# Token rows laid out turned by the host, and modulated there by per-partition columns

## The reference

```python
sh1, sc1, g1, sh2, sc2, g2 = split(silu(c) @ w_mod + b_mod, 6)          # latent tokens
csh1, csc1, ...            = split(silu(c_ctx) @ w_mod + b_mod, 6)      # context tokens
modulate(x, g, shift, scale) = rmsnorm(x, g) * (1 + scale) + shift
h_lat, h_ctx = modulate(x, g_attn, sh1, sc1), modulate(ctx, g_attn, csh1, csc1)
z  = h @ w_in          # columns: q-down 256, kv-down 128, k-rope 32, swa q 512, swa k 128, swa v 128
q_m, k_m, v_m = up-projections of the normed cq, ckv, per-head rmsnorm, rotary
q_s, k_s, v_s = per-head rmsnorm, rotary                                # windowed attention
x = x + g1 * (concat(mla, swa) @ w_out)
x = x + g2 * (relu(modulate(x, g_mlp, sh2, sc2) @ w_mlp1)**2 @ w_mlp2)
```

## Time and profile before

| | us |
|---|---|
| median of three runs | 1400.42 (1398.49 to 1401.47) |
| the profiled execution | 1399.78 |
| its span | 1398.0 |
| TensorE matmul busy | 1357.5 (97%) |
| VectorE busy | 914.6 (65%) |
| ScalarE busy | 692.6 (50%) |
| GpSimd busy | 487.1 (35%) |
| mean granted TensorE clock | 0.988 |

### The profile page before, as it was taken

How to read it: one execution, slowest core, us unless ns; L and a number is a source line. 1 busy time by engine, 2 the same in 40 slices (tenths; PEclk the granted TensorE clock), 3 DMA queues, 4 the chain that set the end, 5 groups by cost and what they waited for, 6 DMA issues and landing times.

```text
span 1398.0 us, 18825 instructions
## 1 busy us (share of the span) xinstructions
PE 1357.5 (97%) x7262; PEld 1149.4 (82%) x7262; DVE 914.6 (65%) x1284; ACT 692.6 (50%) x1343; POOL 487.1 (35%) x321
## 2 busy tenths in 40 slices
PE   5899997999999999999999999999999999999999
PEld 1688987999899988988887888888888888888887
DVE  1878776777777877875774646547564654746463
ACT  2755655788778777972223424333332433333240
POOL 2766553121299992501102303132050323205010
PEclk8999998999999999999999999999999999999999
DMA  9555658433365646301123112121211212121013
GB/s 377 192 162 160 177 159 286 129 89 86 115 199 144 190 131 191 71 1 61 31 76 121 31 31 90 31 75 31 62 44 30 91 31 75 30 62 44 15 61 121
DMA packets 121576, 143.42 MB, mean 103 GB/s; under 512 B 8184, under 2 KB 103288, under 8 KB 118672
## 3 DMA queue, kind: packets, MB, share of 16 engines
q1 hardware_dynamic: 121232, 142.18, 32.6%
q0 software_dynamic: 256, 0.05, 0.0%
HBM read 108.38 MB, written 31.74 MB: 100 GB/s over the span
## 4 chain that ended last, share of the span: by engine, by line
PE 70%; DVE 11%; POOL 7%; ACT 6%; DMA 4%; issue 1%; SPq 1%; DVEq 0%; ACTq 0%; POOLq 0%
PE f_ps L2062 24%; PE f_ps L2331 19%; PE o_ps L1770 6%; PE a_ps L1422 4%; PE a_ps L1438 3%; PE f_ps L2347 3%; POOL l_wg L1349 3%; ACT s_pr L1519 3%; POOL l_gate L1351 3%; PE t_ps L956 2%; PE a_ps L1468 2%; DVE s_nmx L1604 2%; PE t_ps L945 1%; DMA t_wm<-in_w_mod 1%; DMA l_v<-scratch_v 1%
## 5 line engine op out<-in xcount | busy, mean ns | idle before, releaser
L2062 PE MATMUL f_ps<-h,f_w 128*128 128x512 f32 x1536 | 358.0, 389 | 0.4 <-DVE h L1836 0.2
L2062 PEld LDWEIGHTS f_ps<-h,f_w 128*128 128x128 f32 x1536 | 288.1, 188 | 60.7 <-DVE h L1836 0.7
L2261 DVE TENSOR_TENSOR mix<-mix,f_ps 128x512 f32<-128x512 f32 x196 | 128.7, 683 | 152.9 <-PE f_ps L2331 152.9
L2102 POOL TENSOR_TENSOR f_w<-f_w,f_g 128x1024 f32<-128x1024 f32 x30 | 77.0, 2590 | 390.2 <-DMA f_w<-in_w_mlp 342.7
L2139 ACT ACTIVATE f_a<-f_ps 128x512 f32<-128x512 f32 x64 | 38.2, 597 | 254.7 <-PE f_ps L2062 254.7
L2331 PE MATMUL f_ps<-f_bh,f_al 128*128 128x512 f32 x392 | 152.5, 389 | 0.0
L2331 PE MATMUL f_ps<-f_bh,f_ah 128*128 128x512 f32 x392 | 152.5, 389 | 0.0
L2331 PE MATMUL f_ps<-f_bl,f_ah 128*128 128x512 f32 x392 | 152.5, 389 | 0.0
L1618 DVE TENSOR_TENSOR l_pT<-a_ps,l_pT 128x512 fp32r<-128x512 f32 (+1 forms) x192 | 108.9, 594 | 54.0 <-ACT l_pT L1529 53.9
L1422 PE MATMUL a_ps<-l_k,l_q 96*128 96x512 f32 (+1 forms) x576 | 136.5, 366 | 1.6 <-DMA l_v<-scratch_v 1.1
L956 PE MATMUL t_ps<-w_in,t_h 128*128 128x416 f32 (+2 forms) x600 | 125.7, 355 | 0.3 <-DVE w_in L719 0.3
(11 more groups left out here) (223 smaller groups left out, 2425.1 us busy)
## 6 DMA issues: line engine op xcount, KB each, us to landing
l_wg<-in_w_mod SPq DMA_DIRECT2D x8, 2048.0 KB, 8.0
f_w1r<-in_w_mlp SPq DMA_DIRECT2D x32, 512.0 KB, 4.0
f_w<-in_w_mlp SPq DMA_DIRECT2D x16, 1024.0 KB, 5.0
t_wm<-in_w_mod SPq DMA_DIRECT2D x8, 1024.0 KB, 12.5
scratch_k<-t_kT SPq DMA_DIRECT2D x20, 384.0 KB, 3.7
l_k<-scratch_k SPq DMA_DIRECT2D x8, 960.0 KB, 10.6
scratch_q<-t_qT SPq DMA_DIRECT2D x16, 384.0 KB, 3.9
l_q<-scratch_q SPq DMA_DIRECT2D x8, 768.0 KB, 6.3
```

The lines of the kernel that those rows point to most:

```text
L2062: last = nc.tensor.matmul(ps[:, b, :], w1[:, g % 2, w, k, :], h2[x][:, k, half * HB:(half + 1) * HB], start=(k == 0 and i == 0), stop=(k = ...
L2261: V.tensor_tensor(x, x, ps[:, bank_of(i, t), :].rearrange("p (k c) -> p k c", c=P), ALU.add).then_inc(added, 1)
```

## The change

The host also hands over `x_cols`, tiles 1 to 9 of the tokens turned, [128 of the model dimension, 8, 128 tokens]. The rows themselves are still loaded, for the sum of squares. For tiles 1 to 9:

- `load_xT` brings the turned tile into `xT`; its low half `lT` later stands in the same place, so the load of tile i+2 waits for the last product of tile i;
- TensorE turns only the inverse norm, a [128,1] column broadcast to 128 columns: one transposition (fill "x") puts the norms of the 128 tokens on every partition. It stands behind step 6 of `project(i, 1)`, in the order of the banks between sk and c;
- VectorE multiplies the turned tile by that bank (`scale_x`), ScalarE applies scale and shift as per-partition columns, in eight activations of 128x128 (`modulate`), in two groups between k1, q0 and q1, then makes the high copy of 1024 columns (`high_x`), VectorE the low one (`low_x`). GpSimd's shift addition is gone.

Scale and shift come as columns by four transpositions of `mo` and one copy (`mods`); the spreading products and copies are gone. Tile 0 is normed in rows and turned before the last modulation weights arrive, and then modulated on ScalarE (high) and VectorE (low). The product of tile 1 with group 0 stands before `up_kv(0)`. In turn 1, `scale_x(2)` and `low_x(2)` stand on VectorE before the low weights r1 and r2. The output stores use two semaphores in place of four.

```diff
@@ order of the banks
-        turned = [(k, i - 1) for k in (("k0", "k1", "q0", "q1") if lat(i - 1) else ("k0", "k1"))] if i > 1 else []
         here = [("c", i)] if 0 <= i < NT else []
-        order += here + turned if lat(i) else turned + here
-        order += [("x0", i + 1), ("x1", i + 1)] if i + 1 < NT else []
+        ahead = [("x", i + 1)] if 0 < i < NT - 1 else []
+        order += ahead + here if i > 1 else here + ahead
+        order += [(k, i - 1) for k in (("k0", "k1", "q0", "q1") if lat(i - 1) else ("k0", "k1"))] if i > 1 else []
@@ def norm, gain_shift
+    def norm(t):
+        return stx[:, t:t + 1] if t < 2 else inv[:, (t - 2) % 2, 26:27]
+
+    def gain_shift(t, k):
+        m = mods[:, 0 if lat(t) else 1, :]
+        return m[:, 8 + k:9 + k], m[:, k:k + 1]
@@ sync
         def next_x(i):
-            sp.wait_ge(emptied, slot["x1", i] + 1)
+            sp.wait_ge(x_squared, i + 1)
+            if i == 0:
+                sp.wait_ge(emptied, slot["x1", 0] + 1)
             load_x(i + 2)
+
+        def next_xT(i):
+            sp.wait_ge(z_ready, z_at(i) + (3 if lat(i) else 1))
+            load_xT(i + 2)
...
         sp.dma_start(norms[:, :], A["norm_rows"]).then_inc(gains, 16)
+        load_xT(1)
         load_raw("kv")
...
         next_x(0)
+        next_x(1)
...
-        next_x(1)
+        next_xT(0)
         spill_vs(0)
         spill_v(0)
         spill_vs(1)
         spill_rest(0)
+        next_xT(1)
         next_x(2)
         spill_v(1)
         spill_rest(1)
+        next_xT(2)
...
             spill(i - 1)
+            if i < NT - 2:
+                next_xT(i)
@@ scalar
+        def first_high(f):
+
+            if f == 0:
+                act.wait_ge(emptied, 2)
+                act.wait_ge(mod_cols, 1)
+            for k in range(4 * f, 4 * f + 4):
+                g, s = gain_shift(0, k)
+                ins = nc.scalar.activation(hT[0][:, k, :], xT[0][:, k, :], ACT.Identity, scale=g, bias=s)
+            ins.then_inc(h_hi, 1)
...
+        def modulate(t, f):
+
+            if f == 0:
+                act.wait_ge(emptied, slot["x", t] + 1)
+            for k in range(4 * f, 4 * f + 4):
+                g, s = gain_shift(t, k)
+                ins = nc.scalar.activation(xT[t % 2][:, k, :], xT[t % 2][:, k, :], ACT.Identity, scale=g, bias=s)
+            ins.then_inc(h_ready, 1)
+
+        def high_x(t):
+            act.wait_ge(h_ready, 2 * t + 2)
+            nc.scalar.activation(hT[t % 2][:, :, :], xT[t % 2][:, :, :], ACT.Copy).then_inc(h_hi, 1)
@@ scalar, before the loop
         root_x(0)
+        take_first(0)
+        take_first(1)
         high_weights("a0")
         square_x(1, stx[:, 1:2])
+        first_high(0)
+        first_high(1)
+        root_x(1)
         high_weights("a1")
-        hi_fill("x0", 0)
-        hi_fill("x1", 0)
-        root_x(1)
-        for n in range(4):
-            copy_spread(n)
         high_weights("kv")
-        high_weights("r0")
+        modulate(1, 0)
+        modulate(1, 1)
+        high_x(1)
@@ scalar, in the loop
-                if lat(i - 1):
-                    hi_fill("q0", i - 1)
-                    hi_fill("q1", i - 1)
             if i < NT and not lat(i):
                 hi_fill("c", i)
+            if i == 0:
+                high_weights("r0")
+            if 0 < i < NT - 1:
+                modulate(i + 1, 0)
+            if i > 1 and lat(i - 1):
+                hi_fill("q0", i - 1)
+            if 0 < i < NT - 1:
+                modulate(i + 1, 1)
+            if i > 1 and lat(i - 1):
+                hi_fill("q1", i - 1)
+            if 0 < i < NT - 1:
+                high_x(i + 1)
             if lat(i) and i < NT:
                 copy_z(i, 2)
@@ vector
+        def first_low_half(f):
+
+            x = slice(4 * f, 4 * f + 4)
+            if f == 0:
+                dve.wait_ge(emptied, 2)
+            for k in range(4 * f, 4 * f + 4):
+                g, s = gain_shift(0, k)
+                ins = V.tensor_scalar(h_first[:, k, :], xT[0][:, k, :], g, s, ALU.mult, ALU.add)
+            ins.then_inc(h_ready, 1)
+            dve.wait_ge(h_ready, f + 1)
+            dve.wait_ge(h_hi, f + 1)
+            V.tensor_tensor(lT[0][:, x, :], h_first[:, x, :], hT[0][:, x, :].bitcast(F32), ALU.subtract).then_inc(h_lo, 1)
...
         def scale_x(t):
+            dve.wait_ge(filled, slot["x", t] + 1)
+            dve.wait_ge(xT_loaded[t % 2], 16 * ((t + 1) // 2))
+            V.tensor_tensor(xT[t % 2][:, :, :], xT[t % 2][:, :, :], mid(ps[:, slot["x", t] % 2, 0:P], KC), ALU.mult).then_inc(emptied, 1)
+
+        def low_x(t):
+            dve.wait_ge(h_hi, t + 2)
+            V.tensor_tensor(lT[t % 2][:, :, :], xT[t % 2][:, :, :], hT[t % 2][:, :, :].bitcast(F32), ALU.subtract).then_inc(h_lo, 1)
@@ vector, before the loop: first_low_half(0), first_low_half(1), inverse_x(1), scale_x(1), low a1, gains, low kv, low_x(1)
@@ vector, in the loop
-            if 1 < i < NT - 1:
-                scale_x(i + 1)
...
                 lo_fill("sk", i - 1)
+            if 1 < i < NT - 1:
+                scale_x(i + 1)
...
-            if i + 1 < NT:
-                lo_fill("x0", i + 1)
-                lo_fill("x1", i + 1)
+            if i == 1:
+                scale_x(2)
+            if 0 < i < NT - 1:
+                low_x(i + 1)
...
@@ tensor
+            if kind == "x":
+                if t == 1:
+                    pe.wait_ge(x_normed, 2)
+                else:
+                    pe.wait_ge(inv_ready, t - 1)
+                parts = [norm(t).to_broadcast([P, P])]
...
             if i < NT and not lat(i):
                 fill("c", i)
-                fill("x0", i + 1)
-                fill("x1", i + 1)
                 if i == 0:
+                    pe.wait_ge(h_lo, 3)
+                    project(1, 0, {})
                     pe.wait_ge(w_lo, JOBS.index("kv"))
-                    pe.wait_ge(spread_copied, 8)
+                else:
+                    fill("x", 2)
...
+                ahead = {6: ("x", i + 1)} if i + 1 < NT else {}
                 if lat(i - 1):
-                    project(i, 1, {2: ("s", i - 1), 5: ("sk", i - 1)})
+                    project(i, 1, {2: ("s", i - 1), 5: ("sk", i - 1)} | ahead)
...
-                if i + 1 < NT:
-                    fill("x0", i + 1)
-                    fill("x1", i + 1)
@@ output stores: stored[n % 4] becomes stored[n % 2]
```

More of the change, by code:

```diff
@@ L169, in token_phase @@
     cT = [room(f"t_c{i}", [P, 3, P], F32R) for i in range(2)]
-    scale_l = room("t_scale_l", [P, D])
-    shift_l = room("t_shift_l", [P, D])
+    xT = [room(f"t_xT{i}", [P, KC, P]) for i in range(2)]
+    low = Z.room("T", 9984)
+    h_first = Z.room("T", 8192)("t_h_first", [P, KC, P])
+    lT = [low(f"t_l{i}", [P, KC, P], F32R) for i in range(2)]
     junk = room("t_junk", [P, D], mybir.dt.bfloat16)
@@ L177, in token_phase @@
     small = Z.small
+    mods = small("t_mods", [P, 2, 16])
     stx = small("t_stx", [P, 2])
@@ L204, in token_phase @@
     mod_ready = sem("t_mod_ready")
-    spread = sem("t_spread")
-    spread_copied = sem("t_spread_copied")
     w_hi = sem("t_w_hi")
@@ L214, in token_phase @@
     x_root = sem("t_x_root")
-    h_scaled = sem("t_h_scaled")
+    x_normed = sem("t_x_normed")
+    mod_turned = sem("t_mod_turned")
+    mod_cols = sem("t_mod_cols")
+    xT_loaded = [sem(f"t_xT_loaded{i}") for i in range(2)]
     h_ready = sem("t_h_ready")
+    h_hi = sem("t_h_hi")
+    h_lo = sem("t_h_lo")
     filled = sem("t_filled")
@@ L644, in scalar @@
                     square_s(i)
-            if i == 0:
-                for n in range(4, 8):
-                    copy_spread(n)
             if i == 1:
@@ L832, in inverse_x @@
             dve.wait_ge(x_root, t + 1)
+            if t:
+                V.reciprocal(stx[:, t:t + 1], stx[:, t:t + 1]).then_inc(x_normed, 1)
+                return
             link(V.reciprocal(stx[:, t:t + 1], stx[:, t:t + 1]))
+            V.tensor_scalar(xr[:, 0, :], xr[:, 0, :], stx[:, 0:1], None, ALU.mult).then_inc(x_normed, 1)
         link(V.tensor_scalar_add(ex[:, :, :], ex[:, :, :], 1.0))
@@ L855, in vector @@
         low_weights("kv")
+        low_x(1)
         for i in range(NT + 1):
@@ L989, in tensor @@
         for k in range(KC):
+            if k == KC - 1:
+                pe.wait_ge(ident_loaded, 16)
+                fill("x0", 0)
+                fill("x1", 0)
             pe.wait_ge(wm_loaded[k], 16)
@@ L1984, in mlp_phase @@
     added = sem("f_added")
-    stored = [sem(f"f_stored{i}") for i in range(4)]
+    stored = [sem(f"f_stored{i}") for i in range(2)]
     w1_dram = A["w_mlp1"][0].rearrange("(k p) (f c) -> f p k c", p=P, c=P)
@@ L2093, in sync @@
             sp.dma_start(out[0, row * P:(row + 1) * P, dh * HB:(dh + 1) * HB],
-                         fin[:, 2 * row + dh, :]).then_inc(stored[n % 4], 16)
-        for i in range(4):
-            sp.wait_ge(stored[i], 16 * 4)
+                         fin[:, 2 * row + dh, :]).then_inc(stored[n % 2], 16)
```

(2 more changed lines are left out.)

140 lines of the change are left out of this document (45 added, 95 removed).

## The result

The changed kernel takes 1414.47 us (median of 4 runs, 1411.2 to 1415.4), the kernel before 1399.99 beside it (4 runs): 1.0096 times as long, 95% interval 1.0084 to 1.0107. The direction was forecast, the size was not: +14.5 us where the forecast had +5.6, and above the end of the range. The profiled execution spans 1413.2 us against 1398.0.

What follows compares the result with a forecast made beforehand. TensorE was taken to set the settled tile's pace, and VectorE's weight halves the head's chain. Onto 1399.8 us came +1.5 for six tiles and +4.1 for the head, 1405.4, as median 1406.0; range 1399 to 1413.

Steps and rivals of the forecast that it cites:

- x's fill behind s's bank: Settled tile: TensorE waits 1.29 us at x's transposition for s's low halves; net +0.25 us a tile, +1.5 over six.
- fits in the sum: Settled tile: ScalarE rises from 12.3 to 15.4 of 20.3 us with 3.1 us of modulations, and this has room.
- rival A: Faster: if s's low halves finish by TensorE's seventh step, settled tiles lose 8.2 us over six, 1394 us; chance 0.14.
- the late load of x of tile 3: Head: x of tile 3, fetched behind the spill of k of tile 0, lands about 78 us; q-up product at 83.9.
- rival C: Much slower: longer TensorE waits put tiles 1 and 2 at half clock, 5 us more in the head, 1411 us; chance 0.19.
- The head: Before the settled tiles: the first q-up product comes at 84.9 us against 80.84, +4.1 us (+1 to +8).
- The last step: Head, tile 1's scaling to first q-up product: 86.2 at low clock, 83.9 with x of tile 3 late; 84.9 taken.
- Tile 3, forecast a settled tile: Tile 3 counted among six settled tiles (3 to 8), each +0.25 us.
- D: Head: eight modulations under 2.3 us delay tile 2 by 3.4, nearly paid back by the clock, 1400 us; chance 0.24 with B.

Runs made afterwards that it cites:

- e1_sv: The changed kernel with the spill of vs issued ahead of the spills of k and q, no longer behind two x loads: 1410.5 us, ratio 1.0069.
- f3b_square_only: e1_sv with ScalarE's square of the next token rows moved between the high halves of s and sk, x's fill left in place: 1411.03 us, ratio 1.0081.
- e3_both: e1_sv with x's fill first in the bank order and its scaling ahead of the low halves of s, from tile 3 on: 1410.98 us, ratio 1.0072.
- f3_square: e3_both with ScalarE's square of the next token rows moved between the high halves of s and sk: 1405.76 us, ratio 1.0044.
- e4_head: The changed kernel, head reordered: kv-up of tile 0 before tile 1's projection, r1's low half before tile 2's, turned-tile load before tile 0's spills: 1410.68 us, ratio 1.0072.
- e6_mod1: The changed kernel with two 512-column modulation activations a tile instead of eight of 128, scale and shift of six steps left out: 1406.91 us, ratio 1.0052.

## Why the prediction was wrong in size

At tile 9's q-up product the loss is 17.1 us where the forecast had 5.6. The 11.5 between them are 2.9 in the head, 2.3 in tile 3, 4.3 for the spill of vs with the low clock behind it (by e1_sv), and 2.0 over tiles 4 to 8 for the settled tile itself.

- **x's fill behind s's bank: right.** Forecast 1.29 us of idle TensorE and a period of 20.5. With the second chain out of the way (f3b_square_only) TensorE idles 1.07 us (1.28 on the weight loads) and the period is 20.7; the fill stands 12.43 us behind the q-up product, forecast 12.48.
- **The step that failed: ScalarE "fits in the sum".** The forecast charged ScalarE's modulations nothing in the settled tile: 15.4 of 20.3 us (measured 14.9 of 21.0) leave room, and the chain q1, high copy, z, squares, 0.9 us late, was put inside a slack of 1.1. The squares came only 0.63 late, but the same delay moved GpSimd's rotation of s onto the tiny VectorE operation in front of the root, 0.61 more, for which the forecast had no term; rival A even counted on GpSimd holding up nothing any more. The root came 1.24 late. That alone added only 0.2 a tile, but it made a second chain as long as the bank's, so that removing the bank's wait gained only 0.2 (e3_both). Together the two cost 1.1 us a tile (20.92 against f3_square's 19.8): 0.5 of gain and 0.65 of loss in place of +0.25.
- **Missing from the sum: the spill of vs.** The prediction followed the late load of x of tile 3 past SP's queue, but not the spill that now stands behind two loads. It cost 1.5 us in e4_head and, with two falls of the clock, 4.3 in the kernel after. The clock was named in rival C, for the head only.
- **The head, forecast +4.1, measured +7.0** (to 84.9 and 87.56; the forecast took the start before from the chain, 80.84, the timeline has 80.59), with some 1.6 us of scatter. By its own steps: z of tile 0 at 44.1 instead of 43.0; from there to the end of the squares of k 9.5 us instead of 8.1, the products of tile 1 taking 6.2 us instead of 4.5 at a granted clock of 0.50 up to 49 us, which the forecast had only as its upper bound; from there to the low half of tile 2 13.3 (13.4), with VectorE idle 4.3 us in front of it; from there to the q-up product 20.7 (20.4). So 1.1 and 1.4 us were missed ahead of the squares. The last step was right in part by luck: 20.4 was the middle between two ways. On the way that came true, x of tile 3 landing late, the forecast had 19.4 (landing 13.5 us behind the low half, the product 5.9 behind that), and it took 15.2 (82.07) and 5.5.
- **Tile 3, forecast a settled tile, +0.25, measured +2.6.** Eight modulations, high copy and low half of tile 3 stand in line behind the last key copy, 5.5 us (3.18, 1.05, 1.23) against 3.8 us of q- and kv-up products (2.26, 1.55). Moving half of them ahead gained 0.85 in the profile, and the two shorter activations of e6_mod1 1.7.
- **The rivals.** A (faster) needed x's fill without its wait; f3_square is that case, and there the tile does gain 0.5, though the kernel stays 0.4% slower for its head and tile 3. D needed modulations under 2.3 us; they take 3.2. C (1411) lies nearest to the result: its threshold for the tiles, 0.42 us a modulation, was set too high, since at 0.385 the chain was already behind, half of its lateness being the operation that GpSimd held.

## What to carry to other kernels

An engine with a quarter of its time free can still be the longest way round a loop: compare the place of its last result within the period, not its busy share, and ask what its delay moves on the other engines. When removing a wait moves nothing, look at the next instruction that waits; here two ways of equal length hid each other, and only both edits together showed 1.1 us. A new load put in a queue charges everything issued behind it, so follow each of those to the buffer that it frees. A stretch that two engines enter within 0.2 us of each other can come out either way in the next execution; read it in several before you build on it.

## What the runs showed of the hardware

- A tiny VectorE operation was held by GpSimd: `tensor_scalar` on 128x11 took 172 ns at the median before and 776 after, since it now falls into GpSimd's rotation of s. The line's durations after (ns, min/median/max):
```profile
L791 DVE TENSOR_SCALAR t_stn<-t_stn x8: 172/776/801, 95.4 to 243.9; 128x11 f32<-128x11 f32 x8
```
It is 0.6 us of every settled tile's chain to the root. The Trainium skill (SBUF — State Buffer, Who interferes with whom) says that `tensor_scalar` can enter a two-port mode, and that in it whichever issues first, it or GpSimd, blocks the other for the whole instruction; this row agrees, and so do the first four column operations of the head (3.61 us in the rows above, against 1.11 for the next four).
- Which of the two started first decided 3.4 us of VectorE's time in the head: 0.69 us for the addition on 128x512 where it started ahead of GpSimd's subtraction (nine executions), 4.06 to 4.08 where it started 0.15 or 0.16 us behind it (three).
- A 128-column activation with a factor and an offset both from columns follows its like every 0.385 us (eight in 3.18 to 3.19). The forecast took 0.38, its upper bound, and was right: the second column costs as much as the first. The Trainium skill (ScalarE: Activation LUTs, What ACT_TABLE_LOAD costs) gives 186 ns and 0.833 ns an element, 93 for each pointer operand, and 93 of overlap, which makes an estimate of 0.386; the trace agrees.
- TensorE's clock fell to 1.2 GHz (granted 0.50) in two settled tiles of the kernel after, each time behind an idle stretch of 2.0 to 2.1 us at x's fill, and not in e1_sv, where these waits are 1.48 to 1.85. But it stayed at 2.4 GHz (1.00) behind 2.02 and 2.56 us in e4_head, so the length of the stretch alone doesn't decide it. Against e1_sv the two tiles with a low clock took 1.7 and 2.1 us more, part of it the longer wait.
